# Releasing expert slots by the heads' own semaphores, three quarters of one slot earlier, with small work moved between engines

## The reference

```
h  = rms_norm(x, attn_norm_w);  z = h @ w_in       # c_q, c_kv, k_rope, dq, dk, dv, g_mla, g_diff
q  = rms_norm(c_q) @ mla_w_uq;  kv = rms_norm(c_kv) @ mla_w_ukv
o_mla  = softmax(norm_rope(q) @ norm_rope(k).T * s) @ v_mla
a      = softmax(q1 @ k1.T * s + bias) - lam * softmax(q2 @ k2.T * s + bias)
o_diff = rms_norm(a @ v, diff_subln_w) * (1 - lam_init)
merged = sigmoid(g_mla + b0) * o_mla + sigmoid(g_diff + b1) * o_diff
x  = x + merged @ w_out
h2 = rms_norm(x, ffn_norm_w)
gate, idx = top_k(softmax(h2 @ router_w).T, 32)     # per expert
hidden = silu(h2[idx] @ w_gate[e]) * (h2[idx] @ w_up[e])
x  = x + scatter_add(idx, (hidden @ w_down[e]) * gate)
```

## Time and profile before

| | us |
|---|---|
| median of 3 runs | 1473.36 (1473.23 to 1473.41) |
| profiled execution, its own time | 1473.55 |
| its span in the trace | 1471.8 |
| TensorE busy | 1129.7 (77%) |
| VectorE busy | 468.1 (32%) |
| ScalarE busy | 374.7 (25%) |
| GpSimd busy | 49.0 (3%) |
| DMA queue q1: 492.07 MB | 82.4% of 16 engines' span |
| the chain that ended last | DMA 54%, PE 40%, DVE 3% |

### The profile page before, as it was taken

How to read it: one execution, slowest core, us unless ns; L and a number is a source line. 1 busy time by engine, 2 the same in 40 slices (tenths; PEclk the granted TensorE clock), 3 DMA queues, 4 the chain that set the end, 5 groups by cost and what they waited for, 6 DMA issues and landing times.

```text
span 1471.8 us, 20240 instructions
## 1 busy us (share of the span) xinstructions
PE 1129.7 (77%) x8437; PEld 684.3 (46%) x8437; DVE 468.1 (32%) x879; ACT 374.7 (25%) x623; POOL 49.0 (3%) x107
## 2 busy tenths in 40 slices
PE   9999999965656566656656657566566999999998
PEld 8887887521212212212112122122121688999887
DVE  6988885100000000000000000000000478675546
ACT  6658663100001001001001000000100465465434
POOL 1220120000000000000000000000000020000000
PEclk9999999997878968888798687886887999999999
DMA  8663528999999999999999999999999764555551
GB/s 307 200 245 108 206 87 370 420 426 427 427 426 430 428 428 427 427 429 427 426 430 428 427 427 427 428 428 427 430 427 428 294 186 172 172 184 189 196 186 47
DMA packets 58922, 493.33 MB, mean 335 GB/s; under 512 B 6715, under 2 KB 8309, under 8 KB 34165
## 3 DMA queue, kind: packets, MB, share of 16 engines
q1 hardware_dynamic: 58724, 492.07, 82.4%
q10 hardware_dynamic: 144, 0.52, 0.1%
HBM read 491.52 MB, written 1.05 MB: 335 GB/s over the span
## 4 chain that ended last, share of the span: by engine, by line
DMA 54%; PE 40%; DVE 3%; ACT 1%; issue 1%; SPq 0%; ACTq 0%; DVEq 0%
DMA arena<-in_expert_w_down 19%; DMA arena<-in_expert_w_up 18%; DMA arena<-in_expert_w_gate 17%; PE ps L1927 13%; PE ps L2020 7%; PE ps L1932 7%; PE ps L2374 4%; PE ps L2398 2%; PE ps L1999 1%; PE ps L2190 1%; PE ps L2221 1%; DVE w_split L1199 1%; PE ps L1897 1%; PE ps L2134 1%; PE ps L2109 1%
## 5 line engine op out<-in xcount | busy, mean ns | idle before, releaser
L2374 PE MATMUL ps<-ring,arena 128*32 128x512 f32 x1024 | 168.3, 793 | 115.5 <-DMA ring<-in_expert_w_up 60.1
L2374 PE MATMUL ps<-arena 128*32 128x512 f32 x1024 | 163.2, 772 | 115.4 <-DMA arena<-in_expert_w_up 58.6
L1199 DVE TENSOR_TENSOR w_split<-ring,w_split 128x1024 fp32r<-128x1024 f32 (+3 forms) x178 | 201.9, 1141 | 93.6 <-ACT w_split L765 92.3
L765 ACT ACTIVATE w_split<-ring 128x1024 fp32r<-128x1024 f32 (+3 forms) x178 | 175.2, 991 | 180.5 <-PE ps L1932 126.8
L1651 DVE TENSOR_TENSOR arena<-arena,ps 128x512 f32<-128x512 f32 x16 | 11.0, 688 | 557.8 <-PE ps L2374 557.8
L2374 PEld LDWEIGHTS ps<-ring,arena 128*32 128x32 f32 x1024 | 32.9, 127 | 241.5 <-DMA ring<-in_expert_w_up 101.1
L2374 PEld LDWEIGHTS ps<-arena 128*32 128x32 f32 x1024 | 32.7, 126 | 236.0 <-DMA arena<-in_expert_w_up 96.1
L2020 PE MATMUL ps<-hT_hi,w_split 128*128 128x256 f32 x608 | 111.8, 284 | 0.5 <-ACT w_split L765 0.4
L2398 PE MATMUL ps<-arena 128*32 128x256 f32 x1072 | 81.2, 455 | 32.9 <-DMA arena<-in_expert_w_down 27.8
L2398 PE MATMUL ps<-ring,arena 128*32 128x256 f32 x896 | 69.9, 465 | 43.1 <-DMA ring<-in_expert_w_down 40.1
L2020 PEld LDWEIGHTS ps<-hT_hi,w_split 128*128 128x128 f32 x608 | 95.3, 192 | 2.3 <-issue 1.0
...
## 6 DMA issues: line engine op xcount, KB each, us to landing
...
```

The lines of the kernel that those rows point to most:

```text
L765: act.activation(w_split[:, n % WBUFS, 0, 0:cols], slot_view(slot, cols)[:, n % 2, :], ACT.Copy).then_inc(split_hi, 1)
L1199: dve.tensor_tensor(buf[:, 1, :], w, buf[:, 0, :].bitcast(F32), ALU.subtract).then_inc(split_lo, 1)
L2374: m = pe.matmul(ps[j * CAP:(j + 1) * CAP, bank, :], xe[:, kt, :], w[r][:, j * FCOL:(j + 1) * FCOL], start=kt == 0, stop=kt == KT - 1, skip ...
```

## The change

The loader (SyncE's queue) no longer waits for `chunk_used` for chunks 0, 1, 2, 9 (`LAST_ARENA`), 3 and 11 (`HALVED`) but for the heads' outputs (`hO_done`) or the merged transposes (`tr_done`); TensorE's four waits for its own results, with their counts, are gone. Of chunk 2 the first 3072 of 4096 words are loaded once the last head's queries and keys have been transposed (`hT_done`), the rest once all outputs are done. The first half of chunk 12 is loaded as two quarters, released after two and after four products of the first tile. The product with the second gate moves from VectorE to GpSimd as two operations (add one, multiply) on each of two halves. The second batch of small vectors is turned after four tiles of "dq", into bank 6, and copied later. The first low part of "uq0" stands ahead of the angles, and the sums of squares are taken in two halves with the last low part of "uq1" between them. In the second block the squares of the gating unit move from ScalarE to GpSimd, and the high part of tile 2 of "conv" stands ahead of the sigmoids.

```diff
-T1_RELEASES = SLOTS - 2
+T1_RELEASES = 4
...
+        KEYS, KEY_WORDS = 2, 3072
+        all_heads, merged = (hO_done, DHEADS + HEADS), (tr_done, 4 * TRANSPOSED.index("merge") + 4)
+        FREED_BY = {0: (hO_done, DHEADS), 1: (hO_done, DHEADS + IN_GROUP), KEYS: all_heads, LAST_ARENA: all_heads,
+                    3: merged, HALVED: merged}
...
             if n < SLOTS:
-                return T1_ORDER.index(n) + 1
+                return T1_ORDER.index(n) + 1 - len(FREED_BY)
...
-                    sp.wait_ge(first_half_used, 1)
-                    sp.dma_start(slot[:, 0:WIDE // 2], source[:, 0:WIDE // 2]).then_inc(first_half_loaded, 16)
+                    for i in range(2):
+                        words = slice(i * WIDE // 4, (i + 1) * WIDE // 4)
+                        sp.wait_ge(first_quarter_used, i + 1)
+                        sp.dma_start(slot[:, words], source[:, words]).then_inc(first_quarters_loaded, 16)
...
-                sp.wait_ge(chunk_used, slot_free(n))
+                if n in FREED_BY:
+                    sp.wait_ge(*FREED_BY[n])
+                else:
+                    sp.wait_ge(chunk_used, slot_free(n))
+                if n == KEYS:
+                    slot, loaded = expert_slot(n)
+                    sp.dma_start(slot[:, KEY_WORDS:WIDE], chunk_source(0, n)[:, KEY_WORDS:WIDE]).then_inc(loaded, 16)
+                    return
                 load_expert(n)
...
             load_freed(T1_ORDER[1])
+            sp.wait_ge(hT_done, DHEADS + HEADS)
+            sp.dma_start(expert_slot(KEYS)[0][:, 0:KEY_WORDS], chunk_source(0, KEYS)[:, 0:KEY_WORDS]).then_inc(keys_loaded, 16)
...
-            pool.sem_inc(od_ready, 1)
+            for c in range(2):
+                pool.wait_ge(gate_ready, HALVES + c + 1)
+                g, od = (b[:, :, c * 512:(c + 1) * 512] for b in (gb, dq))
+                step(pool.tensor_scalar(g, g, 1.0, None, ALU.add))
+                pool.tensor_tensor(od, od, g, ALU.mult).then_inc(od_gated, 2)
...
+            pool.wait_ge(gelu_done, 4)
+            pool.wait_ge(sq_read, 7)
+            gating = cv2.rearrange("p h d -> p (h d)")
+            pool.tensor_tensor(sq[:, 0:HALVES * SGU], gating, gating, ALU.mult).then_inc(sq_ready, 1)
             pool.wait_ge(sq_read, 8)
...
             gelus(1)
-            act.wait_ge(gelu_done, 4)
-            act.wait_ge(sq_read, 7)
-            act.activation(sq[:, 0:HALVES * SGU], cv2.rearrange("p h d -> p (h d)"), ACT.Square).then_inc(sq_ready, 1)
+            high_parts("conv", 2, 3)
             act.activation(lam_s[:, 0:1], rstd_0[:, 0:1], ACT.Sigmoid)
             act.wait_ge(stick_cleared, 1)
             sigmoids(0)
-            high_parts("conv", 2, 3)
...
             low_parts("dq", 0, 1)
-            dve.wait_ge(vec_done, 2)
-            dve.tensor_copy(ffn_vec[:, :].rearrange("p (c r) -> p r c", r=IN_ROWS),
-                            ps[:, 0, NVEC:NVEC + KT].rearrange("p (r c) -> p r c", r=IN_ROWS)).then_inc(ffn_vec_ready, 1)
-            dve.tensor_copy(vec[:, KT:NVEC], ps[:, 0, KT:NVEC]).then_inc(vec_ready, 1)
             evac("c", (c_sb[:, 1, :].rearrange("p (j c) -> p j c", j=2), two_pieces))
-            dve.wait_ge(vec_ready, 2)
-            dve.scalar_tensor_tensor(qk_w, vec[:, VEC["diff_q_hnorm_w"]:VEC["diff_q_hnorm_w"] + 1], DQK ** -0.5,
...
             low_parts("dq", 3, 5)
+            dve.wait_ge(vec_done, 2)
+            dve.tensor_copy(vec[:, KT:NVEC], ps[:, 6, KT:NVEC]).then_inc(vec_ready, 1)
+            dve.tensor_copy(ffn_vec[:, :].rearrange("p (c r) -> p r c", r=IN_ROWS),
+                            ps[:, 6, NVEC:NVEC + KT].rearrange("p (r c) -> p r c", r=IN_ROWS)).then_inc(ffn_vec_ready, 1)
+            dve.wait_ge(vec_ready, 2)
+            step(dve.scalar_tensor_tensor(qk_w, vec[:, VEC["diff_q_hnorm_w"]:VEC["diff_q_hnorm_w"] + 1], DQK ** -0.5,
...
             low_parts("dq", 7)
+            low_parts("uq0", 0, 1)
...
-            low_parts("uq0", 0, 1)
             evac("dq", (dq[:, 1, :], whole))
...
-            diff_sums(0)
+            dve.wait_ge(sq_ready, 1)
+            step(dve.tensor_reduce(ss_d[:, 0:HEADS], sq[:, 0:D].rearrange("p (n d) -> p n d", d=DQK), AX, ALU.add))
             low_parts("uq1", 1)
+            head_sums(0, sq[:, D:2 * D].rearrange("p (n d) -> p n d", d=DQK), ss_d[:, HEADS:2 * HEADS])
             evac("uq0", (q[:, 0, 1, :], whole))
...
-                if HEADS - 6 < i <= HEADS - 2:
-                    gate_outputs(i - HEADS + 5)
...
             tiles("c", hT, ready=lambda kt: stage_high("attn", kt), low_ready=lambda kt: stage_ready("attn", kt))
+            tiles("dq", hT, range(0, 4))
             pe.wait_ge(vec_loaded, 16 * N_VEC)
...
-            pe.transpose(ps[:, 0, 0:NVEC], vec_rows[:, :], ident[0:NVEC, 0:NVEC]).then_inc(vec_done, 1)
-            pe.wait_ge(vec_ready, 2)
-            pe.wait_ge(ffn_vec_ready, 1)
-            tiles("dq", hT, range(0, 4))
             pe.wait_ge(c_norm, 4)
             out_of_psum("c")
...
+            pe.transpose(ps[:, 6, 0:NVEC], vec_rows[:, :], ident[0:NVEC, 0:NVEC]).then_inc(vec_done, 1)
...
             tiles("dq", hT, range(4, KT))
+            pe.wait_ge(vec_ready, 2)
+            pe.wait_ge(ffn_vec_ready, 1)
...
-            pe.wait_ge(hO_done, DHEADS)
-            pe.sem_inc(chunk_used, 1)
...
-                if i == IN_GROUP + 3:
-                    pe.wait_ge(hO_done, DHEADS + IN_GROUP)
-                    pe.sem_inc(chunk_used, 1)
...
-            pe.wait_ge(hO_done, DHEADS + HEADS)
-            pe.sem_inc(chunk_used, 2)
...
-            pe.wait_ge(tr_done, 4 * TRANSPOSED.index("merge") + 4)
-            pe.sem_inc(chunk_used, 2)
...
-                            if first and bank == 0 and kt == 0:
-                                m.then_inc(first_half_used, 1)
+                                if first and bank == 0 and kt == 0 and j % 2:
+                                    m.then_inc(first_quarter_used, 1)
```

24 lines of the change are left out of this document (10 added, 14 removed).

## The result

The changed kernel takes 1475.24 us (median of 20 runs, 1473.96 to 1476.87) against 1472.88 for the kernel before beside it (20 runs, 1472.07 to 1475.01): 2.4 us more, ratio 1.0015 [1.0009, 1.0021]. It was forecast 1.8 us faster. The profiled execution took 1474.77, its span is 1472.9.

What follows compares the result with a forecast made beforehand. The expert-weight stream was taken to bound the kernel, its end fixed by the compute chain to chunk 12's issue. Terms +0.9 - 1.5 - 0.6 - 0.43 - 0.2 = -1.8 us gave 1471.5; range 1470.6 to 1473.4, with rivals 1469.0 to 1473.8.

Steps and rivals of the forecast that it cites:

- start: Small vectors and low parts ahead of "ukv0": VectorE stands for the later turns and "ukv0" starts later, +0.9 us (0.2 to 1.2).
- drains: TensorE's four waits for its own results, at the heads and "out": removing them gives -1.5 us, at least -0.9.
- gate products: Second gate's product moved to GpSimd: TensorE's idle of 0.59 ahead of the merge goes, -0.6 us (-0.3 to -0.6).
- quarters: First half of chunk 12: first quarter released after two products of the first tile rather than four, -0.43 us (0 to -0.43).
- the expected overlap with a two-input operation is near nothing: Gate products: each releasing tanh ends just as VectorE's low part of "out" does, so GpSimd's operations hardly meet two-input work.
- The rival of GpSimd holding VectorE: Each of GpSimd's four new operations holds VectorE for its whole length, 6.0 us: +4.2 in all, 1477.5; chance 0.06.
- the maxima between 195 and 205: Sign to watch on VectorE: the forecast is wrong if these maxima come late.
- the one in the middle: The fourth removed wait, in the middle of the heads, has other work issued behind it: 0.1 us (0 to 0.47).
- The early load: Three quarters of chunk 2 loaded early, 1.57 MB: at most 3.67 us, worth some 0.5, counted inside the sum.
- Gap forecast at 246 to 248.6: DMA engines idle there after the early load, taking 2.6 us of the 3.67; the forecast is wrong without this dip.
- it lets the chain's gain through: Without the early load the stream's bytes would last to 264.4, against chunk 12 at 264.3 less the quarter's part.
- The second block: After the stream, TensorE's idle of 0.39 for the high part of tile 2 of "conv": -0.2 us (-0.4 to 0).

Runs made afterwards that it cites:

- x2: Changed kernel with the start as before (vectors turned ahead of "dq", old order of low parts, one reduction): 2.1 us less than the changed kernel.
- y1: Kernel before with only the loader's semaphores changed, TensorE's four waits gone: 0.64 us less than before.
- y4: y1 with the gate products on GpSimd: 1.1 us more than y1.
- z2: y2 with the first half of chunk 12 loaded as two quarters: within 0.1 us of y2.
- w4: w1 with the gates' first add as two operations, its second in two pieces; looked at for durations alone: first add 1.04 us instead of 2.77.
- z4: y2 with gate products on GpSimd and VectorE's low parts 1 and 2 of "out" behind them: last output 0.63 us earlier than y2; its time isn't given.
- w2: Changed kernel with VectorE's low parts 1 and 2 of "out" moved behind GpSimd's four operations: 2.85 us less than the changed kernel, 0.5 less than before.
- y3: y2 with the second block's part, the changed order of low parts and the split sum: last output 0.16 us later than y2; its time isn't given.
- w3: w1 with the small vectors turned later and copied on VectorE behind the position work: same time as w1, output 0.41 us later.
- v1: w3 with VectorE's vector copies in the middle of the position work: output 0.24 us earlier than w1, time against before 0.2 lower than w1's.
- x1: Changed kernel with the gate products back on VectorE as four operations: 2.2 us less than the changed kernel.
- z3: y2 with the second block's part (squares on GpSimd, high part of tile 2 of "conv" ahead of the sigmoids): 0.8 us less than y2.
- x4: Changed kernel with chunk 2 loaded whole when all heads are done: 0.5 us less than the changed kernel.
- y2: y1 plus the early load of three quarters of chunk 2: 1.05 us less than before, 0.4 less than y1.
- w1: z4 with the second block's part: 1471.00 us against 1472.94 for the kernel before.
- v2: w1 with chunk 2 loaded whole: 0.9 us more than w1.
- x3: Changed kernel with the first half of chunk 12 in one transfer: 1.0 us less than the changed kernel.

## Why the prediction was wrong, by its own steps

Up to the issue of chunk 12 the terms can be read off the chain. Measured: start +1.2 (x2), drains -1.4 (y1), gate products +1.4 (y4), quarters 0 (z2): +1.1 or +1.2, and the changed kernel's mark is 243.17 - 242.04 = +1.13. The sum was made in the right way; two of its terms were wrong, one of them in sign.

**The gate products, forecast -0.6, measured +1.38.** This is the step that failed: "the expected overlap with a two-input operation is near nothing". The release was read rightly: each tanh ends as a low part of "out" does. The lengths were not: 1.11 for the add and 1.90 for the multiplication, 3.0 us a pair. The pair takes 2.77 and 2.36, 5.3 us from the start of the add to the end of the multiplication, and the four operations, taken as 6.0, last 11.2. The low parts of "out", two SBUF inputs each, stood here in the kernel before (one more at 194.16), and the two tanh that release the pairs end at 195.1 and 200.4:

```profile
199.32 1.22 DVE L1199 TENSOR_TENSOR w_split<-ring,w_split 128x1024 fp32r<-128x1024 f32 x1
...
204.49 1.22 DVE L1199 TENSOR_TENSOR w_split<-ring,w_split 128x1024 fp32r<-128x1024 f32 x1
```

Pairs of 3.0 would have ended at 198 and 203.4, each ahead of the next low part, so by its own lengths the forecast was consistent. Pairs of 5.3 reach across both. Both durations were read off the wrong row: 1.11 belongs to an add with a second operation (L703, add and multiply), and for two whole operands the scaling by a row just behind L717 was nearer than L717 with its broadcast:

```profile
190.69 2.36 POOL L718 TENSOR_TENSOR arena<-arena,row 128x1024 f32<-128x1024 f32 x1
```

By w4 a pair with the two-operation add would take some 3.6 us from the first start to the last end and could fit between the low parts where they were; that is worked out, no run has it. The rival of GpSimd holding VectorE had the mechanism and priced it at 6.0 for full overlap; the two meetings cost 2.0 (z4 against y4, w2 against the changed kernel). The place where VectorE held TensorE, the maxima between 195 and 205, was the right one to watch.

The other terms:

- **The start, +0.9 forecast, +1.2 measured.** Mechanism right (1.21 of stand, where about 1 was forecast, and the loss reappears ahead of "ukv0"), and 1.2 was its upper bound. 0.16 is the split sum (y3), which had been called neutral. That the cost is who waits for the copies, and not the turns' place, is shown by w3 and v1.
- **The drains, -1.5.** Right: -0.44 at the heads (the 0.47 there leaves nothing for the one in the middle) and -0.99 at "out", -1.43 in all.
- **The quarters, -0.43.** Nothing: the four products of one tile run side by side (z2), which was the bound of 0 in the prediction. The term took them one behind the other. What had no bound was a cost. Take for each kernel its time against before less its issue's shift (stars less 0.4). The five with early load and quarters (the changed kernel, x1, x2, z2, w2) give 1.2, 0.4, 0.3, 0.4, 0.4, mean 0.55; the nine with early load and a half give -0.4 to 0.7, mean 0.1. So some 0.4, at the edge of chance, and 0.2 without the changed kernel itself.
- **What goes with the quarters.** The windows are sharper than the times. Take the thirteen windows of one us from the one ahead of chunk 12's issue on, and count each as missing 1 less its rate over 428 GB/s. The five took 1.15 to 1.43 us to issue the rest of the chunk (0.33 in the kernel before), show a second dip of 184 to 201 GB/s, and miss 2.1 to 2.5 us. Of the ten executions with early load and a half (w4 too) eight issued it in 0.33 and miss 1.2 to 1.6; the two that issued it as slowly, z3 (1.43) and z4 (1.14), miss 2.3 and 2.4. So the loss of about 1 us of stream goes with the slow issue, and the quarters, all five of them against two of ten, with it. x4, with quarters and without the early load, issued it in 0.39 and misses 0.9. Why the issue is slow stays open. The times don't settle it: of the nine with a half, z3 has the lowest time for its chain and z4 the highest.
- **The early load.** Gap forecast at 246 to 248.6, found at 248 to 251, shifted as the chain is. "2.6 us of the 3.67 turn into an idle gap": from 243 us to the last of those thirteen the windows miss 2.6 us more in y2 than in y1 and 2.7 more in w1 than in v2, so 1.0 us of the bytes stays a gain; 3.1 more in the changed kernel than in x4. In the times, with a half and no early load (y1, y4, v2) time less shift is 0.8, 0.5 and 0.9, mean 0.75, against 0.1 with it. "Worth some 0.5 us" was right in its sign and rather low. That "it lets the chain's gain through" fits y1 and v2, but y4, whose chain gained almost nothing, stands 0.5 above its shift as well. In the changed kernel none of it is seen in the time (x4), within chance.
- **The second block, -0.2.** Nothing, 318.2 to the end of the span either way. Its bound of 0.

With the 0.4 that the other four kernels with early load and quarters have above their chains, the changed kernel should be 1.13 + 0.4 = 1.5 us slower. 2.4 was measured, with an interval from 1.3 to 3.1. The 0.8 that is left stays open. Each of x1, x2 and w2 gave back 0.8 to 0.9 more than its chain, and x3 1.0 with no gain on it, whatever was undone. All of them are held against the one measurement of the changed kernel, which was taken on another occasion than theirs and not repeated, so chance in that one number, or a difference of the occasion, would explain all four. An effect of the whole change on the stream behind chunk 12 isn't ruled out.

The changed kernel has a sound part, the semaphores and the early load, and the forecast saw it. What it moved to GpSimd and what it turned later each met a collision that its own order makes, and moving a few instructions on VectorE removes each (z4 and w2; v1).

The Trainium skill (SBUF — State Buffer, "Who interferes with whom") states that a VectorE instruction with two SBUF inputs contends with a GpSimd instruction that reads SBUF, that the port they share is an exclusive lock, and that a VectorE instruction with at most one SBUF input, outside its 2-port modes, does not contend. The trace agrees: VectorE's low part ends 1.08 behind the end of GpSimd's instruction twice, and there is no effect on the maxima, copies and scalings. An estimate from that page: each meeting costs VectorE at most the length of one of GpSimd's instructions, so what counts is how many two-input instructions fall among them. Here the two meetings lengthened the low parts by 1.10 and 1.23; each met an instruction of 2.36.
